# Half of an input product as seven block products per chunk in place of eight, with the rounding of the weight blocks shared by two engines

## The chip, the cores and the metric

One core of a Trainium2 chip runs the whole program. The metric is the device time in microseconds, a median over runs. Engines: TensorE (PE) multiplies, VectorE (DVE), ScalarE (ACT) and GpSimd (POOL) work on elements, SyncE (SP) issues the transfers.

## The reference

Two residual blocks on x of shape (1, 1024, 1024), all in float32. The first is the one touched:

```python
u = rms_norm(h, norm_in_g[l])
proj = jnp.einsum('bsd,de->bse', u, w_in[l])
pool_x, pool_z, m_x, m_z = jnp.split(proj, [D_POOL, 2 * D_POOL, 2 * D_POOL + D_MLSTM], axis=-1)
y_pool = pool_mixer(pool_x, pool_w[l], pool_scale[l]) * jax.nn.silu(pool_z)
y_m = mlstm_branch(m_x, ...) * jax.nn.silu(m_z)
y = jnp.concatenate([y_pool.astype(h.dtype), y_m.astype(h.dtype)], axis=-1)
h = h + jnp.einsum('bse,ed->bsd', y, w_out[l])
```

`pool_mixer` takes four groups of 256 features; in each it forms a centred window mean (over 2, 4, 8 or 16 positions) minus the value itself, and multiplies by a 256x256 matrix. The second block (gating, a 31-tap convolution, windowed attention) is not touched.

## The kernel before

Every large product is made in three passes. A float32 factor is split into a high part, rounded to the format that TensorE takes (`fp32r`), and a low part, the rest. `three` issues low x high, high x low and high x high into one PSUM bank, each a matmul of 128x512 columns.

Weights come in chunks of 256 output features, 1 MB each, into the one buffer `wraw` (`wt`, SP). GpSimd rounds a chunk into `whi` (L687) and subtracts it into `wlo` (L689), function `split`; both have two buffers. The pool half of `w_in` is eight chunks, two per group g: chunk 2g gives `pool_x` and chunk 2g+1 gives `pool_z`. For each, `group` makes four tiles (two of 128 features, two halves of 512 positions), each a sum over eight blocks k of 128 inputs: 4 x 8 x 3 = 96 matmuls.

The order around it is written out by hand in each engine's program, with semaphores between them:

- TensorE: chunk 0 in a special order (`lagging`, while x is still being transposed), then per g the chunks 2g and 2g+1 and the mixing, 4 x 2 x 3 = 24 matmuls, then the output product over y (chunks 8 to 11, 96 matmuls each), then chunk 12 (`W_MX`) and the rest.
- ScalarE: copies the tiles of chunk 2g out of PSUM to `px`, applies silu to those of chunk 2g+1 (`sz`), and rounds the pooled values and y.
- VectorE: at the start it scales x (L1511) and makes the low parts of u (L1520). Per g it forms the windows (L1555 to L1561, on `px`, in `pta` and `ptb`), the low parts of the mixing's factors (L1565, L1569), scales the mixing's result (L1578) and makes the low part of y (L1586).
- y lies as `yp_hi` and `yp_lo` in SBUF from the mixing to the output product, in the place where x was and, for the low part, beside it.

## Time and profile before

| | before |
|---|---|
| median of 3 runs | 1170.21 us (1169.76 to 1170.4) |
| span of the profiled execution | 1168.5 us |
| TensorE busy | 1158.7 us, 99% |
| TensorE weight loads | 946.1 us, 81%, beside the matmuls |
| VectorE busy | 678.5 us, 58% |
| GpSimd busy | 455.9 us, 39% |
| ScalarE busy | 359.2 us, 31% |
| DMA | 93.56 MB, 80 GB/s in the mean |

The span runs from the first to the last instruction; the profiled execution has no time of its own beside it, and the median of the runs lies 1.7 us above the span. A matmul's record ends later than the next one starts, so the pace of TensorE is read from the starts. The granted clock of TensorE is at its full level (2.4 GHz) in all 40 slices of the page.

### The profile page before, as it was taken

Reading aid. Unit: us, or ns where it says so; the run is one execution under the profiler, and the core shown is the slowest. Engines: PE = TensorE matmul, PEld = TensorE weight load, DVE = VectorE, ACT = ScalarE, POOL = GpSimd, SP = SyncE. Lnnn points to the kernel's source line nnn. Section 1 sums busy time; section 2 is a strip of 40 time slices with the busy share of each in tenths; the row PEclk is TensorE's granted clock in tenths of the full one; section 3 lists DMA queues with packets and bytes.
Section 4 is the critical chain, followed back from the end, with each engine's and each line's share of the span. In section 5 each row is a group of like instructions: output and inputs, shape, how many; then the busy total and the mean of one; then the engine's idle time right before and its main releaser. Section 6 shows DMA issues by size and latency. Waiting matters only on the chain.

```text
span 1168.5 us, 17252 instructions
## 1 busy us (share of the span) xinstructions
PE 1158.7 (99%) x6599; PEld 946.1 (81%) x6599; DVE 678.5 (58%) x1249; ACT 359.2 (31%) x720; POOL 455.9 (39%) x437
## 2 busy tenths in 40 slices
PE   9999999999999999999999999999999999999997
PEld 6888888888888868888878888878988887777786
DVE  5645557334368502157777883894699434556668
ACT  6312121100012212445665631242111134553322
POOL 2424222223333223354657656304223323455534
PEclk9999999999999999999999999999999999999999
DMA  7321121343312112300113242123121130133113
GB/s 241 109 81 45 36 81 36 123 152 114 109 36 72 64 64 90 101 23 23 50 34 112 88 171 73 72 100 95 40 88 36 37 100 1 38 122 124 39 38 141
DMA packets 75075, 93.56 MB, mean 80 GB/s; under 512 B 13938, under 2 KB 54090, under 8 KB 74483
## 3 DMA queue, kind: packets, MB, share of 16 engines
q1 hardware_dynamic: 67270, 88.73, 22.7%
q10 hardware_dynamic: 7724, 3.74, 1.2%
q8 instruction: 53, 0.87, 0.3%
q14 instruction: 28, 0.22, 0.1%
HBM read 75.11 MB, written 18.92 MB: 80 GB/s over the span
## 4 chain that ended last, share of the span: by engine, by line
PE 93%; DVE 4%; DMA 1%; ACT 1%; issue 1%; POOL 0%; ACTq 0%; DVEq 0%; POOLq 0%
PE bank L918 22%; PE bank L920 22%; PE bank L919 22%; PE bank L1219 4%; PE bank L1194 4%; PE wide L1210 2%; PE wide L1412 2%; PE bank L1158 1%; PE bank L1147 1%; PE bank L1135 1%; PE wide L920 1%; PE wide L919 1%; PE wide L918 1%; PE bank L1387 1%; DVE h L1910 1%; PE wide L1387 1%
## 5 line engine op out<-in xcount | busy, mean ns | idle before, releaser
L687 POOL CAST whi<-wraw 128x2048 fp32r<-128x2048 f32 x31 | 58.8, 1898 | 454.1 <-PE bank L920 404.1
L918 PE MATMUL bank<-u_hi,wlo 128*128 128x512 f32 x488 | 190.4, 390 | 0.0
L920 PE MATMUL bank<-u_hi,whi 128*128 128x512 f32 x488 | 189.9, 389 | 0.0
L919 PE MATMUL bank<-u_lo,whi 128*128 128x512 f32 x488 | 189.9, 389 | 0.0
L689 POOL TENSOR_TENSOR wlo<-wraw,whi 128x2048 fp32r<-128x2048 f32 x32 | 153.1, 4784 | 3.0 <-ACT whi L2488 0.5
L918 PE MATMUL bank<-x_hi,wlo 128*128 128x512 f32 x312 | 123.5, 396 | 0.0
L920 PE MATMUL bank<-x_hi,whi 128*128 128x512 f32 x312 | 121.6, 390 | 0.0
L919 PE MATMUL bank<-x_lo,whi 128*128 128x512 f32 x312 | 121.5, 389 | 0.0
L918 PEld LDWEIGHTS bank<-u_hi,wlo 128*128 128x128 f32 x488 | 91.6, 188 | 19.9 <-POOL wlo L689 0.8
L920 PEld LDWEIGHTS bank<-u_hi,whi 128*128 128x128 f32 x488 | 91.6, 188 | 19.0
L919 PEld LDWEIGHTS bank<-u_lo,whi 128*128 128x128 f32 x488 | 91.6, 188 | 18.9
L918 PEld LDWEIGHTS bank<-x_hi,wlo 128*128 128x128 f32 x312 | 58.5, 188 | 16.1 <-issue 4.3
L1990 DVE SCALAR_TENSOR_TENSOR wide<-glu,VT,wide 128x1024 f32<-128x1024 f32 x58 | 69.3, 1281 | 0.0
L920 PEld LDWEIGHTS bank<-x_hi,whi 128*128 128x128 f32 x312 | 58.5, 188 | 12.4
L919 PEld LDWEIGHTS bank<-x_lo,whi 128*128 128x128 f32 x312 | 58.6, 188 | 11.7
L862 POOL TENSOR_SCALAR sp<-sp,rcx 128x384 f32<-128x384 f32 (+1 forms) x64 | 37.9, 606 | 76.4 <-DVE rcx L2077 76.4
L1219 PE MATMUL bank<-v,kwb 128*128 128x257 f32 x224 | 58.3, 383 | 0.5 <-DVE Cst L1773 0.3
L1650 DVE SCALAR_TENSOR_TENSOR cva<-um,VT,cva 128x1022 f32<-128x1022 f32 (+1 forms) x32 | 58.0, 1812 | 1.1
L1194 PE MATMUL bank<-Cst,qT 128*128 128x257 f32 x224 | 58.0, 381 | 0.1
L2296 ACT ACTIVATE um<-bank 128x512 f32<-128x512 f32 x16 | 9.6, 599 | 155.7 <-PE bank L920 155.7
L783 POOL TENSOR_TENSOR Pm<-ST,Wb 128x128 f32<-128x128 f32 x64 | 29.1, 455 | 66.0 <-ACT Wb L2368 61.2
L918 PE MATMUL bank<-whi,ym_lo 128*128 128x512 f32 x128 | 51.2, 400 | 0.0
(391 smaller groups left out, 2440.9 us busy)
## 6 DMA issues: line engine op xcount, KB each, us to landing
wraw<-in_w_in SPq DMA_DIRECT2D x26, 1024.0 KB, 5.5
wraw<-in_w_out SPq DMA_DIRECT2D x12, 1024.0 KB, 5.1
xr<-in_x SPq DMA_DIRECT2D x8, 512.0 KB, 7.3
hst<-in_x SPq DMA_DIRECT2D x4, 1024.0 KB, 5.0
hpool<-hst SPq DMA_DIRECT2D x4, 1024.0 KB, 4.1
smz<-mzs SPq DMA_DIRECT2D x16, 256.0 KB, 2.0
h<-hpool SPq DMA_DIRECT2D x4, 1024.0 KB, 7.5
resid<-h SPq DMA_DIRECT2D x8, 512.0 KB, 2.6
```

The lines of the kernel that those rows point to most:

```text
L687: g_.tensor_copy(whi[w % 2][:, :, :], wraw[:, :, :]).then_inc(s["w_hi"], 1)
L689: g_.tensor_tensor(wlo[w % 2][:, :, :], wraw[:, :, :], whi[w % 2][:, :, :].bitcast(F32), ALU.subtract).then_inc(s["w_lo"], 1)
L783: g_.tensor_tensor(Pm[:, n % 2, :], STs[h % 2][:, ck, :], Wb[:, n % 2, :], ALU.mult).then_inc(s["g_P"], 1)
L862: g_.tensor_scalar(row, row, rcx[:, x % 2, i:i + 1], 0.5 if g else 1.0, ALU.mult, ALU.mult).then_inc(s["g_nm"], 1)
L918: pe.matmul(ps, al, bh, start=(k == 0), stop=False)
L919: pe.matmul(ps, ah, bl, start=False, stop=False)
L920: return pe.matmul(ps, ah, bh, start=False, stop=(k == nk - 1))
L1194: mm = pe.matmul(ps[:, 0:AUG], q[:, k, ck * P:(ck + 1) * P], Cst[:, d, k, :], start=(k == 0), stop=(k == 1))
L1210: pe.matmul(ps[:, 0:AUG], Pm[:, n % 2, :], v[:, ck, :], start=True, stop=True).then_inc(s["t_intra"], 1)
L1219: mm = pe.matmul(ps[:, 0:AUG], kwb[:, m % 2, k * P:(k + 1) * P], v[:, ck, :], start=True, stop=True)
L1650: ins = ve.scalar_tensor_tensor(acc[:, a0:a1], um[:, j, a0 + sh:a1 + sh], tap(q), acc[:, a0:a1], ALU.mult, ALU.add)
L1990: ins = ve.scalar_tensor_tensor(dst, src, w, acc, ALU.mult, ALU.add)
```

## The change

For chunks 1 to 7 (`SEVEN`), a product of two by two blocks is made of seven block products. The blocks are those of the inputs (k 0 to 3 and 4 to 7, called 0 and 1), of the features (two of 128) and of the positions (two halves of 512). Each product has inner length 4 x 128 and makes 4 x 3 = 12 matmuls: 84 a chunk. Three of the seven use the halves of u as they are (0 and 1 in the first half, 1 in the second), four use sums and differences of them, `Tf`, made once. Of the seven weight blocks, three are blocks of the raw weights, which ScalarE rounds; four are sums and differences or one raw difference, which GpSimd forms and rounds itself; the low parts of all seven are GpSimd's. VectorE adds the seven results to four tiles (`add_up`, one operand in PSUM, `p1s` or `p5s` in SBUF). Slots for eight blocks lie in the old weight buffers.

To make room, y is stored to DRAM when it is made (`store_y`) and read back before the output product (`load_y`); four blocks of u's second half are parked in DRAM too (`late_d`). A chunk's weights come as two halves of 512 KB (`halves`), each when its place in `wraw` is free. The mixing of group g now comes after the second product of chunk 2g+2; that of group 3 after chunk 7.

```diff
+    for w, (_, _, layout) in enumerate(plan):
+        first.append(first[-1] + (0 if w in SEVEN else size[layout]))
...
+            def halves(c, f):
+
+                if c == 1:
+                    sp_.wait_ge(s["w_lo"], 1)
+                else:
+                    sp_.wait_ge(s["w_lo"] if f else s["g_m0"], c if f else c - 1)
...
+            for c in range(2, 8):
+                for f in range(2):
+                    halves(c, f)
+                if c % 2:
+                    g = (c - 3) // 2
+                    store_y(g)
+                    sp_.wait_ge(s["t_mix"], 4 * g + 4)
+                    mix_weights(g + 1)
+            wt(W_OP)
...
-            g_.wait_ge(s["v_xn"], NT)
-            for w in range(1, W_MX + 2):
+            g_.wait_ge(s["v_ulo"], 8)
+            for n in range(2):
+                ks = slice(4 * n, 4 * n + 4)
+                g_.tensor_tensor(Tf[:, 2 + n, :, :], u_hi[:, ks, 0:HALF].bitcast(F32), u_lo[:, ks, 0:HALF].bitcast(F32),
+                                 ALU.add).then_inc(s["g_T"], 1)
...
+            def seven(c):
+
+                b0 = 7 * (c - 1)
+
+                def low(i, src):
+                    return g_.tensor_tensor(slot(wlo, b0 + i), src, slot(whi, b0 + i).bitcast(F32), ALU.subtract)
...
+                for k in range(2):
+                    g_.wait_ge(s["a_wa"], 3 * c - 2 + k)
+                    low(k, raw(0, k)).then_inc(s["g_blk"], 1)
+                g_.wait_ge(s["l_wraw"], 16 * (c + 1))
+                x = xs[:, :, :]
+                step(g_.tensor_tensor(x, raw(1, 0), raw(1, 1), ALU.add))
+                step(g_.tensor_tensor(raw(1, 0), raw(0, 0), raw(1, 0), ALU.subtract))
+                part(2, x).then_inc(s["g_blk"], 1)
+                g_.wait_ge(s["g_blk"], 6 * (c - 1) + 3)
+                step(g_.tensor_tensor(x, x, raw(0, 0), ALU.subtract))
+                part(3, x).then_inc(s["g_blk"], 1)
+                g_.wait_ge(s["g_blk"], 6 * (c - 1) + 4)
+                g_.tensor_tensor(x, raw(0, 1), x, ALU.subtract).then_inc(s["g_m0"], 1)
+                g_.wait_ge(s["g_m0"], c)
+                part(4, x).then_inc(s["g_blk"], 1)
+                part(5, raw(1, 0)).then_inc(s["g_blk"], 1)
+                g_.wait_ge(s["a_wa"], 3 * c)
+                low(6, raw(1, 1)).then_inc(s["w_lo"], 1)
...
+            def seven(c):
+
+                b0, v0 = 7 * (c - 1), 7 * (c - 1)
+                features = lambda k, nh: [u[:, 4 * k:4 * k + 4, nh * HALF:(nh + 1) * HALF] for u in (u_hi, u_lo)]
+                combined = lambda i: [T[:, i, :, :] for T in (Thi, Tlo)]
+                factors = (features(0, 0), features(1, 0), combined(0), combined(1), features(1, 1), combined(2),
+                           combined(3))
...
+                    if i < 6:
+                        pe.wait_ge(s["g_blk"], 6 * (c - 1) + i + 1)
+                    else:
+                        pe.wait_ge(s["w_lo"], c + 1)
+                    if c == 1 and i in LATE_T:
+                        pe.wait_ge(s["v_Tlo"], LATE_T[i])
+                    wh, wl = slot(whi, b0 + i), slot(wlo, b0 + i)
+                    for k in range(4):
+                        mm = three(ps[:, :], ((wh[:, k, :], wl[:, k, :]), (moving[0][:, k, :], moving[1][:, k, :])),
+                                   k, 4)
+                    mm.then_inc(s["t_prod"], 1)
+                    if i == 1 and c % 2 == 0:
+                        mix(c // 2 - 1)
...
+            ve.wait_ge(s["v_ulo"], 16)
+            whole(0, 0)
+            ve.wait_ge(s["g_T"], 2)
+            combine(0, full(0), full(2), ALU.subtract)
+            whole(1, 1)
+            combine(1, full(1), full(0), ALU.subtract)
+            low_T(0)
+            combine(2, full(1), full(2), ALU.subtract)
+            combine(3, full(3), full(1), ALU.subtract)
+            low_T(1)
...
+            for c in SEVEN:
+                g = c // 2
+                if c < 7:
+                    high_block(c + 1, 0)
+                if c > 1:
+                    keep(c)
+                if c < 7:
+                    high_block(c + 1, 1)
```

GpSimd after its first subtractions, before the change: one cast and one subtraction of 2048 columns for each chunk (L708 and L702 belong to chunk 0).

```order
L702 TENSOR_TENSOR wlo<-wraw,whi 128x2x128 x4
L687 CAST whi<-wraw 128x2048
L689 TENSOR_TENSOR wlo<-wraw,whi 128x2048
L687 CAST whi<-wraw 128x2048
L689 TENSOR_TENSOR wlo<-wraw,whi 128x2048
```

The same place after the change: first the two additions for `Tf` (L807), then the first eleven operations for chunk 1 (L822 low parts, L830 casts, L838 to L845 sums and differences of weight blocks in `xs`).

```order
L807 TENSOR_TENSOR Tf<-u_hi,u_lo 128x2048 x2
L822 TENSOR_TENSOR wlo<-wraw,whi 128x512 x2
L838 TENSOR_TENSOR xs<-wraw 128x512
L839 TENSOR_TENSOR wraw<-wraw 128x4x128
L830 CAST whi<-xs 128x512
L822 TENSOR_TENSOR wlo<-xs,whi 128x512
L842 TENSOR_TENSOR xs<-xs,wraw 128x512
L830 CAST whi<-xs 128x512
L822 TENSOR_TENSOR wlo<-xs,whi 128x512
L845 TENSOR_TENSOR xs<-wraw,xs 128x512
L830 CAST whi<-xs 128x512
L822 TENSOR_TENSOR wlo<-xs,whi 128x512
```

Two operations of 2048 columns per chunk became fifteen of 512, and two of 2048 stand ahead of them. VectorE at the end of u's low parts, before:

```order
L1511 TENSOR_SCALAR xr<-xr,rs 128x1024
L1520 SCALAR_TENSOR_TENSOR u_lo<-wide0,VT,u_hi 128x512 x2
L1520 SCALAR_TENSOR_TENSOR u_lo<-wide1,VT,u_hi 128x512 x2
L1520 SCALAR_TENSOR_TENSOR u_lo<-wide0,VT,u_hi 128x512 x2
L1520 SCALAR_TENSOR_TENSOR u_lo<-wide1,VT,u_hi 128x512 x2
L1539 COPY VT<-wide0 128x144
L1555 TENSOR_TENSOR pta<-px 128x1055
L1559 TENSOR_TENSOR pta<-pta,cst 128x8
L1560 TENSOR_TENSOR pta<-pta,cst 128x8
```

And after, up to the first window for group 0 (L1742 makes the four `Tf`, L1751 their low parts, L1735 is `add_up`):

```order
L1695 SCALAR_TENSOR_TENSOR u_lo<-wide1,VT,u_hi 128x512 x2
L1742 TENSOR_TENSOR Tf<-u_hi,u_lo 128x2048
L1742 TENSOR_TENSOR Tf<-Tf 128x2048
L1742 TENSOR_TENSOR Tf<-u_hi,u_lo 128x2048
L1742 TENSOR_TENSOR Tf<-Tf 128x2048
L1751 TENSOR_TENSOR Tlo<-Tf,Thi 128x2048
L1742 TENSOR_TENSOR Tf<-Tf 128x2048 x2
L1751 TENSOR_TENSOR Tlo<-Tf,Thi 128x2048
L1766 COPY VT<-wide0 128x144
L1735 TENSOR_TENSOR sz<-wide1,p1s 128x512
L1751 TENSOR_TENSOR Tlo<-Tf,Thi 128x2048 x2
L1822 TENSOR_TENSOR pta<-px 128x1055
```

Ten operations of 2048 columns stand between the last low part of u and the first window. VectorE ahead of the mixing of group 3, before (L1555 to L1561 the windows of the second 128 features, then the low parts; L1578 follows the mixing):

```order
L1555 TENSOR_TENSOR pta<-px 128x1055
L1555 TENSOR_TENSOR ptb<-pta 128x1053
L1555 TENSOR_TENSOR pta<-ptb 128x1049
L1555 TENSOR_TENSOR ptb<-pta 128x1041
L1559 TENSOR_TENSOR ptb<-ptb,cst 128x8
L1560 TENSOR_TENSOR ptb<-ptb,cst 128x8
L1561 SCALAR_TENSOR_TENSOR px<-ptb,px 128x1024
L1565 TENSOR_TENSOR pwlo<-pw,pwhi 128x512
L1569 TENSOR_TENSOR yp_lo<-px,yp_hi 128x1024 x2
L1578 SCALAR_TENSOR_TENSOR yr<-wide,VT,sz 128x512 x2
```

The same place after the change, with `add_up` of chunk 7 (L1735) between the windows and the low parts:

```order
L1822 TENSOR_TENSOR pta<-px 128x1055
L1822 TENSOR_TENSOR ptb<-pta 128x1053
L1735 TENSOR_TENSOR sz<-wide,p1s 128x512
L1822 TENSOR_TENSOR pta<-ptb 128x1049
L1822 TENSOR_TENSOR ptb<-pta 128x1041
L1829 TENSOR_TENSOR ptb<-ptb,cst 128x8
L1830 TENSOR_TENSOR ptb<-ptb,cst 128x8
L1831 SCALAR_TENSOR_TENSOR px<-ptb,px 128x1024
L1837 TENSOR_TENSOR pwl<-pw,pwhi 128x512
L1841 TENSOR_TENSOR pxl<-px,u_hi 128x1024
L1735 TENSOR_TENSOR p5s<-wide,p1s 128x512
L1735 TENSOR_TENSOR p1s<-wide,p5s 128x512
```

The windows are the same. What moved: the mixing's low parts (now `pwl` and `pxl`) stand among the additions of chunk 7's products, one of which (L1735) is already inside the windows, and the mixing waits for the second `pxl`.

## Rows read from the trace of the kernel before

**Rows 1.** The page: span and busy time of each engine

```profile
span 1168.5 us, 17252 instructions
...
PE 1158.7 (99%) x6599; PEld 946.1 (81%) x6599; DVE 678.5 (58%) x1249; ACT 359.2 (31%) x720; POOL 455.9 (39%) x437
```

**Rows 2.** TensorE's waits, longest first: who for, us, times, longest

```profile
PE bank L960 <- POOL eps L694: 1.0, 1, 1.0
```

**Rows 3.** TensorE's timeline: start us, us, engine, line, what

```profile
41.09 0.47 PE L918 MATMUL bank<-u_hi,wlo 128*128 128x512 f32 x1
...
209.85 0.39 PE L918 MATMUL wide<-yp_hi,pwlo 128*128 128x512 f32 x1
...
214.61 0.39 PE L918 MATMUL wide<-yp_hi,pwlo 128*128 128x512 f32 x1
```

**Rows 4.** GpSimd's timeline, in three stretches

```profile
43.26 5.50 POOL L689 TENSOR_TENSOR wlo<-wraw,whi 128x2048 fp32r<-128x2048 f32 x1
63.27 1.89 POOL L687 CAST whi<-wraw 128x2048 fp32r<-128x2048 f32 x1 [14.51 <-PE bank L920]
65.24 4.61 POOL L689 TENSOR_TENSOR wlo<-wraw,whi 128x2048 fp32r<-128x2048 f32 x1
...
835.83 4.61 POOL L689 TENSOR_TENSOR wlo<-wraw,whi 128x2048 fp32r<-128x2048 f32 x1
...
1015.43 0.61 POOL L843 CAST whi<-wraw 128x512 fp32r<-128x512 f32 x1
1016.13 1.27 POOL L846 TENSOR_TENSOR wlo<-wraw,whi 128x512 fp32r<-128x512 f32 x1
```

**Rows 5.** VectorE's timeline, in two stretches

```profile
41.92 2.37 DVE L1555 TENSOR_TENSOR pta<-px 128x1055 f32<-128x1055 f32 x1 [0.29 <-ACT px L2241]
44.33 4.46 DVE L1559 TENSOR_TENSOR pta<-pta,cst 128x8 f32<-128x8 f32 x1
48.82 0.17 DVE L1560 TENSOR_TENSOR pta<-pta,cst 128x8 f32<-128x8 f32 x1
...
65.89 0.75 DVE L1578 SCALAR_TENSOR_TENSOR yr<-wide,VT,sz 128x512 f32<-128x512 f32 x1 [0.53 <-PE wide L920]
66.56 3.85 DVE L1586 TENSOR_TENSOR yp_lo<-yr,yp_hi 128x512 fp32r<-128x512 f32 x1
...
71.11 0.68 DVE L1586 TENSOR_TENSOR yp_lo<-yr,yp_hi 128x512 fp32r<-128x512 f32 x1
...
837.60 2.87 DVE L1997 TENSOR_SCALAR v_<-mv 128x8 f32<-128x8 f32 x1
```

**Rows 6.** The timeline of all engines at the start

```profile
19.93 0.74 POOL L702 TENSOR_TENSOR wlo<-wraw,whi 128x256 fp32r<-128x256 f32 x1
...
20.44 0.78 DVE L1511 TENSOR_SCALAR xr<-xr,rs 128x1024 f32<-128x1024 f32 x1
...
21.81 0.76 DVE L1511 TENSOR_SCALAR xr<-xr,rs 128x1024 f32<-128x1024 f32 x1
...
23.59 0.48 PEld L1026 LDWEIGHTS wide<-cst,xr 128*128 128x128 f32 x3
...
25.31 0.49 PEld L1026 LDWEIGHTS wide<-cst,xr 128*128 128x128 f32 x3
...
34.02 1.08 ACT L2241 ACTIVATE px<-bank 128x512 f32<-128x512 f32 x2
```

**Rows 7.** VectorE's groups by shape, 0 to 330 us: count | busy, mean ns

```profile
L1569 DVE TENSOR_TENSOR yp_lo<-px,yp_hi 128x1024 fp32r<-128x1024 f32 x8 | 9.5, 1219 | 0.2 <-ACT yp_hi L2279 0.2
...
L1555 DVE TENSOR_TENSOR ptb<-pta 128x1041 f32<-128x1041 f32 x2 | 2.5, 1247 | 0.1
```

**Rows 8.** The page's DMA issues: KB each, us to landing

```profile
wraw<-in_w_in SPq DMA_DIRECT2D x26, 1024.0 KB, 5.5
...
smz<-mzs SPq DMA_DIRECT2D x16, 256.0 KB, 2.0
```

**Rows 9.** DMA issues from 0 to 330 us

```profile
wraw<-in_w_in SPq DMA_DIRECT2D x2, 512.0 KB, 10.2
```

More of the change, by code:

```diff
@@ L104, in chunk_plan @@
     return plan
+SEVEN = range(1, 8)
 def build(nc, I, out):
@@ L110, in build @@
     first = [0]
-    for _, _, layout in plan:
-        first.append(first[-1] + size[layout])
+    for w, (_, _, layout) in enumerate(plan):
+        first.append(first[-1] + (0 if w in SEVEN else size[layout]))
     NCH = len(plan)
@@ L235, in build @@
         (_k, vrow, vrow2, junk, relst, hot,
-         px, pta, ptb, sz, yr, pw, pwhi, pwlo,
+         px, pta, ptb, sz, yr, pw, pwhi, xs,
+         pxl, _z, yl, pwl,
          hst,
@@ L527, in _ @@
                 load_h(0, q)
+            wt(W_OP + 1)
+            store_y(3)
+            for i in range(2):
+                sp_.wait_ge(s[f"o_y{i}"], 256)
+            sp_.wait_ge(s["t_prod"], products + 7)
+            load_y(4, slice(0, S), "l_yc")
+            load_y(6, slice(0, S), "l_yc")
+            sp_.wait_ge(s["v_sum"], 7 * len(SEVEN))
+            for part, (u, sl) in enumerate(((u_hi, slice(0, 4)), (u_lo, slice(0, 4)))):
+                sp_.dma_start(u[:, sl, HALF:S].bitcast(F32), late_d[:, part, :, :]).then_inc(s["l_late"], 16)
             wt(W_OP + 2)
@@ L833, in _ @@
                 split(w)
-            parts = [7]
             def split_part(w, part):
@@ L1556, in _ @@
                         src = dst
+                        if g and step == 1:
+                            for i in (0,) if m else (4, 5, 6):
+                                add_up(2 * g + m, i)
                     tot = src[:, PAD - left:PAD - left + S]
@@ L1596, in fold_gates @@
                         ve.wait_ge(s["l_wg"], 16 * 12)
+                        ve.wait_ge(s["w_lo"], W_OP)
+                        for i in range(2):
+                            ve.wait_ge(s[f"o_y{i}"], 256)
                     w = wn[:, :, :, :].rearrange("p n j o -> p (n j o)").unsqueeze(2).to_broadcast([P, 96, 8])
@@ new lines, in _ @@
+            for k in range(2):
+                high_block(1, k)
+            for i in range(3):
+                pooled(0, i)
+            high_T(0)
+            high_T(1)
+            pooled(0, 3)
+            ac.wait_ge(s["o_late"], 32)
+            high_T(2)
+            high_last(1)
+            high_T(3)
+            keep(1)
+            for c in SEVEN:
+                g = c // 2
+                if c < 7:
+                    high_block(c + 1, 0)
+                if c > 1:
+                    keep(c)
+                if c < 7:
+                    high_block(c + 1, 1)
+                if c % 2 == 0:
+                    for n in range(4):
+                        high_y(4 * (g - 1) + n)
+                    high_last(c + 1)
+                    continue
+                ac.wait_ge(s["l_pw"], 16 * (g + 1))
@@ L2288, in conv_silu @@
+                if c < 7:
+                    high_last(c + 1)
+            for n in range(12, 16):
+                high_y(n)
             def conv_silu(j):
```

354 lines of the change are left out of this document (251 added, 103 removed).

## The prediction

> **What bounds the kernel now.** Read the page first: TensorE is busy for 1158.7 of 1168.5 us [rows 1]. The list of waits is next: TensorE's longest wait anywhere is 1.0 us, at the very start [rows 2]. Then its timeline: from 209.85 to 214.61 us there are 21 steps between starts, 0.2267 us for each 128x512 matmul [rows 3] (the 389 ns of a record is the modelled, overlapping length, so only starts count). So TensorE's instruction count sets the end, at 0.2267 us a piece, as long as nobody makes it wait. The question is what the change takes off that count, and whether the other engines still deliver in time.
>
> **What is removed.** Seven chunks go from 4 groups x 8 x 3 = 96 matmuls to 7 products x 4 x 3 = 84. That is 84 fewer, 84 x 0.2267 = **19.0 us**. The mixing products (24 a pair of chunks) stay. A chunk now takes 19.0 us, a product 2.72, a mixing 5.4; a pair of chunks with its mixing 43.5.
>
> **What is added, and the resource that it needs.** GpSimd did one cast (63.27: 1.89 us) and one subtraction (65.24: 4.61 us) per chunk [rows 4]. Now it does 11 two-input operations and 4 casts of 128x512 each. Rows of that size, late in the program, have 0.61 and 1.27, and I take 1.28 with the step between two [rows 4]: 11 x 1.28 + 4 x 0.61 = 16.5 us a chunk, 33.0 a pair. That alone is under TensorE's 43.5. What matters is with whom it is shared. At 44.33 VectorE starts an addition of 8 columns, whose twin at 48.82 takes 0.17 us; it takes 4.46 us and ends at 48.79, just when GpSimd's subtraction ends (43.26 + 5.50 = 48.76) [rows 4, 5]. At 66.56 a subtraction that takes 0.68 us when free (71.11) takes 3.85 and ends 0.56 us after GpSimd's (65.24 + 4.61 = 69.85). It goes the other way too: GpSimd's 4.61 is 5.50 where VectorE was in an operation until 44.29 (41.92 + 2.37). But the operation at 65.89, which reads PSUM, keeps its 0.75 us inside the same GpSimd subtraction. So operations of VectorE whose operands all lie in SBUF and GpSimd's operations exclude one another, for their whole length; one that waited is shortened by about 0.13 us (0.56 for 0.69; 48.76 - 44.29 = 4.47 for 4.61).
>
> The Trainium skill states this in "SBUF — State Buffer", section "SBUF: two separate sides": a port pair that the two engines share is an exclusive lock, and whichever starts first has it for the whole instruction. By that rule without the 0.13 us, the waits below would sum to about 15 us more, and the time would be some 1218 us. The trace agrees with the rule but for those 0.13 us, and the sum goes by the trace.
>
> I therefore wrote down the five engines' instructions of the stage in the new order, each with its duration from these rows and started when its semaphores allow, and gave the port to whoever asked first. Each place where TensorE waits is a term.
>
> *a. Start.* GpSimd's two 2048-column additions follow its first subtractions, at 20.67 (19.93 + 0.74) [rows 6]. VectorE is scaling x just then: its 0.78 us operation at 20.44 holds the port until 21.2, the addition runs to 25.7, and the scaling that was issued at 21.81 ends at 26.3. TensorE wants that tile at 23.59: **2.7 us**. The second addition runs to 30.8, the next scaling to 31.4; TensorE, 2.7 us late, is there at 28.0: **3.3 us**. The last tile comes in time. Whether a scaling, one input in SBUF, is held too, no row in this stretch shows; the bound below is 0. I take the full price, since a one-input operation of 8 columns, started at 837.60, lasts 2.87 us, to the end of GpSimd's subtraction of 835.83 [rows 4, 5].
>
> *b. Chunk 1.* It started at 41.1 [rows 3], now at 47.1; its fifth product would start at 47.1 + 4 x 2.72 = 58.0. That product needs GpSimd's twelfth operation. GpSimd starts when ScalarE is through (34.02 [rows 6] + 6.0 + 0.6 = 40.6), and from there it alternates with VectorE's ten 2048-column operations (two of 1.22 [rows 7], less one overhead, give 2.25 each) and one window. So 9 x 1.28 + 3 x 0.61 + 10 x 2.25 + 1.25 = 37.1, less 22 handovers x 0.13 = 34.2: ready at 74.8. **16.8 us** of waits, spread over products 3 to 5. Bounds: 1.8 us if the port were free, some 20 without the 0.13.
>
> *c. Chunks 2 to 7.* In a pair VectorE needs, all from SBUF: two windows of g+1 additions (1.25 each), small edges (0.17), one scaling of 1024 (1.23), pwl (0.69), two pxl (1.22) and four yl (0.69) [rows 5, 7], 14.0, 16.5 and 19.0 us for g = 1, 2, 3. With GpSimd's 33.0 that is 47.0, 49.5 and 52.0, less 34 to 42 handovers x 0.13 = 42.6, 44.6, 46.5, against TensorE's 43.5. The 14 additions of products read PSUM, so they don't ask for the port (0.69 each, the length of the twin from SBUF), but they queue behind operations that do. There is no slack left, so each late result shows: chunk 2 waits 1.9 and 5.4 us for its first product to be copied and added up, since ScalarE is held by a weight half still in flight and VectorE by what it left from chunk 1; chunks 4 and 6 wait 0.4 + 1.4 and 3.6 for the mixing's operands. **12.7 us**. I took 4.0 us for the landing of a 512 KB half, between 2.0 (256 KB) and 5.5 (1 MB) [rows 8]; at 3.0 the total is 3.6 us less, at 5.5 it is 5 us more.
>
> *d. The last mixing.* Chunk 7 ends, and the windows for g = 3 have only begun with that chunk: 13.1 us of port time for windows, 3.1 for the low parts, 9 of additions, and GpSimd's last blocks and the first 4.6 us subtraction for the output product between them. **11.5 us**. Before, the same windows lay beside a whole chunk, with GpSimd's 6.5 us.
>
> *e. y by way of memory.* y is now stored and read back. The first half is read during chunk 7. Of the second, four reads of 1 MB follow the last stores; at about 2.9 us each in a queue (the 5.5 us of one alone, less the part that overlaps, an estimate) they land some 4.6 us after TensorE has spent its 21.8 us on the first output chunk. **4.6 us**, bounds 0 and 10. ScalarE's three casts per chunk (0.6 us each, as its two copies in 1.08 us at 34.02 [rows 6]) don't use the port and lie beside TensorE's 19 us: nothing; put on GpSimd they would add 1.8 us of port a chunk.
>
> *Sum:* 6.0 + 16.8 + 12.7 + 11.5 + 4.6 = 51.6 us of waits, less 19.0: +32.6. The span would be 1168.5 + 32.6 = 1201.1; the median of the runs, 1170.21, lies 1.7 above the span, and I keep that: **1203 us**.
>
> **The rivals.** *R1, only the start and the end show* (0.15): in the steady stretch whoever asks does not lose as much as I think, and c and d fall away to about 0 and 4. Then 6.0 + 16.8 + 4 + 4.6 - 19.0 = +12, or with the start's 6.0 absent too, +6: 1176 to 1183. For it: port time and TensorE time are nearly equal in c (42.6 to 46.5 against 43.5). Against it: d's windows come last whatever the pairs do. *R2, faster* (0.13): the two engines seldom meet, because their requests interleave in the gaps that each has at semaphores. The same order without any exclusion leaves waits of 1.8 us in chunk 1 and 4.6 for y, 6.4 - 19.0 = -12.6: 1157.6 us. It decides the sign once all waits together stay under 19.0 us, that is, if less than four tenths of mine come true. Against it: the ten 2048-column operations and GpSimd's twelve stand in one stretch with nothing else to do, b alone is 16.8. *R3, transfers* (0.07): 512 KB halves in 512-byte pieces land as late as the two at the start, whose median is 10.2 us [rows 9], and GpSimd stands idle for each: 12 halves, of whose extra 6 us about a third is hidden, over +20 on top: 1222 and above. *R4, no change* (0.02): waits happen to be 19.
>
> **How the numbers follow.** My own case has 0.63, with 1184 to 1222 as its range: the waits at the low side (handover 0.2 us, halves in 3 us, nothing for y) sum to 33, at the high side (no handover gain, halves in 5.5) to 71. Adding R1 brings the range to 1174 to 1222, which holds 0.78. A measurement of this kernel can tell 0.2% (2.3 us) from no change. Faster than that: R2, 0.13. Within: 0.02. Slower: 0.63 + 0.15 + 0.07 = 0.85.
>
> **What would show it.** In the profile of the changed kernel: TensorE's waits should sum to about 50 us, with 2 to 4 us each on the scaled x at 24 to 31 us (a), on GpSimd's blocks in chunk 1 (b), and a single wait over 8 us on pxl before the last mixing (d). VectorE's 2048-column operations should last about 3.3 us from issue, not 2.25, and GpSimd's 512-column ones in 41 to 75 us over 3 us. The matmuls should be 84 fewer at the same 0.2267 us. I am wrong if VectorE's operations from SBUF run at their own length beside GpSimd's (then R2), if chunk 1 ends before about 70 us, or if the longest waits are on transfers (R3).

## The result and the profile after

| | before | after |
|---|---|---|
| median | 1170.31 us (1169.76 to 1170.95, 4 runs) | 1215.25 us (1213.83 to 1217.47, 4 runs) |
| profiled execution | span 1168.5 us | 1216.29 us, span 1214.5 us |
| mean granted clock of TensorE | 0.999 | 0.976 |

The ratio is 1.0389, 95% interval 1.0374 to 1.0404: 44.9 us slower where 33 were forecast. First the page of the changed kernel, to be read beside [rows 1]: the span, the busy times, TensorE's 40 slices and those of its granted clock.

```profile
span 1214.5 us, 17418 instructions
...
PE 1160.2 (96%) x6515; PEld 942.2 (78%) x6515; DVE 762.9 (63%) x1308; ACT 373.1 (31%) x732; POOL 577.4 (48%) x530
...
PE   8878999687999999999999999999999999999997
...
PEclk9878999898999999999999999999999999999999
```

The 84 matmuls are gone (6599 to 6515), and still TensorE is busy as long as before. TensorE's two dips (slices 2 to 4 and 8 to 10) lie in the first ten slices, and its granted clock falls in five of these six. Next TensorE's list of waits, which had a longest entry of 1.0 us before [rows 2]: who waits for whom, us in total, times, longest. `PE bank L1057 <- DVE pxl` is a matmul that writes `bank` and waited for VectorE's `pxl`.

```profile
PE bank L1057 <- DVE pxl L1841: 11.2, 2, 10.2
PE bank L1057 <- DMA yp_lo<-ylow: 8.9, 1, 8.9
PE bank L1057 <- POOL wlo L822: 7.3, 2, 3.7
PE wide L1057 <- POOL wlo L822: 5.1, 1, 5.1
PE wide L1165 <- DVE xr L1686: 4.9, 2, 2.6
PE wide L1057 <- DVE px L1735: 4.8, 1, 4.8
PE wide L1057 <- issue: 3.4, 1, 3.4
```

These ten waits sum to 45.6 us. But a wait is not all that is lost at its place, because matmuls behind it run slower. What is lost is read from starts. This is TensorE's timeline at the ends of the prediction's five terms: chunk 1 begins, its product 5 (the last late one) begins, the third mixing, the last mixing, the second output chunk, and the first matmul of `W_MX`.

```profile
48.06 0.47 PE L1057 MATMUL wide<-u_hi,wlo 128*128 128x512 f32 x1
...
76.23 0.77 PE L1057 MATMUL bank<-u_hi,wlo 128*128 128x512 f32 x1 [3.60 <-POOL wlo L822]
...
188.41 0.50 PE L1057 MATMUL bank<-u_hi,pwl 128*128 128x512 f32 x1 [0.98 <-DVE pxl L1841]
...
237.11 0.80 PE L1057 MATMUL bank<-u_hi,pwl 128*128 128x512 f32 x1 [10.23 <-DVE pxl L1841]
...
281.21 0.79 PE L1057 MATMUL bank<-whi,yp_lo 128*128 128x512 f32 x1 [8.92 <-DMA yp_lo<-ylow]
...
349.22 0.39 PE L1057 MATMUL bank<-u_hi,wlo 128*128 128x512 f32 x1
```

Between two of them, the elapsed time less 0.2267 us for each matmul is the loss. Chunk 1 began at 41.09 before [rows 3]; `W_MX` began at 302.33, by TensorE's timeline in the kernel before:

```profile
302.33 0.39 PE L918 MATMUL bank<-u_hi,wlo 128*128 128x512 f32 x1
```

| term | stretch | matmuls | lost | forecast |
|---|---|---|---|---|
| a start | to 48.06 | as before | 7.0 | 6.0 |
| b chunk 1 | to 76.23 | 48 | 17.3 | 16.8 |
| c chunks 2 to 7 | to 188.41 | 444 | 11.5 | 12.7 |
| d last mixing | to 237.11 | 168 | 10.6 | 11.5 |
| e y by way of memory | to 349.22 | 408 | 19.6 | 4.6 |

The sum is 66.0, less 19.0 for the 84 matmuls: +47.0, and `W_MX` began 46.9 us later. The third mixing stands inside chunk 6, so what chunks 6 and 7 lose behind it is booked under d. Four terms came within 1.2 us of their forecast; e is 15 us too small. The mechanism that carries a to d can be seen directly, at the start and in chunk 1. VectorE's timeline (answering to [rows 5, 6]):

```profile
20.23 0.75 DVE L1686 TENSOR_SCALAR xr<-xr,rs 128x1024 f32<-128x1024 f32 x1
...
21.60 4.36 DVE L1686 TENSOR_SCALAR xr<-xr,rs 128x1024 f32<-128x1024 f32 x1
...
26.07 4.84 DVE L1686 TENSOR_SCALAR xr<-xr,rs 128x1024 f32<-128x1024 f32 x1
...
48.47 3.28 DVE L1742 TENSOR_TENSOR Tf<-u_hi,u_lo 128x2048 f32<-128x2048 f32 x1
51.78 3.26 DVE L1742 TENSOR_TENSOR Tf<-Tf 128x2048 f32<-128x2048 f32 x1
55.07 2.58 DVE L1751 TENSOR_TENSOR Tlo<-Tf,Thi 128x2048 fp32r<-128x2048 f32 x1
...
67.08 0.69 DVE L1735 TENSOR_TENSOR sz<-wide,p1s 128x512 f32<-128x512 f32 x1
```

And GpSimd's in the same stretch, against [rows 4], where such operations take 0.61 and 1.27:

```profile
41.70 4.58 POOL L822 TENSOR_TENSOR wlo<-wraw,whi 128x512 fp32r<-128x512 f32 x2 [11.34 <-ACT whi L2527]
46.25 3.34 POOL L838 TENSOR_TENSOR xs<-wraw 128x512 f32<-128x512 f32 x1
49.67 3.22 POOL L839 TENSOR_TENSOR wraw<-wraw 128x512 f32<-128x512 f32 x1
52.95 2.55 POOL L830 CAST whi<-xs 128x512 fp32r<-128x512 f32 x1
...
62.13 2.55 POOL L830 CAST whi<-xs 128x512 fp32r<-128x512 f32 x1
64.76 3.19 POOL L822 TENSOR_TENSOR wlo<-xs,whi 128x512 fp32r<-128x512 f32 x1
```

The two engines take turns: each operation lasts as long as its own work and that of the other engine which ran first. One pair takes 3.30 us (48.47 to 51.78 to 55.07). The addition `sz<-wide,p1s`, one operand in PSUM, keeps its 0.69 us inside GpSimd's operation of 64.76.

### The profile page after: what moved, and what is told of

Its sections match the earlier page's. It is cut to its first block, busy times and chain, and to the rows that moved or that the text cites. A ratio compares the mean times of both kernels' runs of the same rounds, so it can differ in the third digit from the quotient of the medians.

```text
span 1214.5 us, 17418 instructions
## 1 busy us (share of the span) xinstructions
PE 1160.2 (96%) x6515; PEld 942.2 (78%) x6515; DVE 762.9 (63%) x1308; ACT 373.1 (31%) x732; POOL 577.4 (48%) x530
## 4 chain that ended last, share of the span: by engine, by line
PE 78%; DVE 10%; POOL 5%; DMA 3%; issue 2%; ACT 1%; SPq 1%; DVEq 0%; ACTq 0%; POOLq 0%
PE bank L1057 19%; PE bank L1059 18%; PE bank L1058 18%; PE bank L1369 3%; PE bank L1394 3%; DMA ylow<-yl 2%; PE wide L1385 2%; PE wide L1587 2%; DVE pta L1822 1%; POOL wlo L822 1%; DVE px L1831 1%; DVE ptb L1822 1%; DVE yl L1788 1%; PE bank L1333 1%; PE bank L1322 1%
## 5 line engine op out<-in xcount | busy, mean ns | idle before, releaser
L779 POOL CAST whi<-wraw 128x2048 fp32r<-128x2048 f32 x24 | 45.5, 1894 | 353.8 <-PE bank L1059 284.2
L1057 PE MATMUL bank<-x_hi,wlo 128*128 128x512 f32 x312 | 123.5, 396 | 0.0
L1057 PE MATMUL bank<-u_hi,wlo 128*128 128x512 f32 x300 | 118.3, 394 | 3.6 <-POOL wlo L822 3.6
L781 POOL TENSOR_TENSOR wlo<-wraw,whi 128x2048 fp32r<-128x2048 f32 x25 | 117.2, 4688 | 2.4 <-ACT whi L2804 0.5
L1059 PE MATMUL bank<-u_hi,whi 128*128 128x512 f32 x300 | 117.7, 392 | 0.0
L1058 PE MATMUL bank<-u_lo,whi 128*128 128x512 f32 x300 | 117.7, 392 | 0.0
L1057 PEld LDWEIGHTS bank<-x_hi,wlo 128*128 128x128 f32 x312 | 58.6, 188 | 16.1 <-issue 4.3
L1057 PEld LDWEIGHTS bank<-u_hi,wlo 128*128 128x128 f32 x300 | 56.8, 189 | 16.6 <-issue 4.0
L1059 PEld LDWEIGHTS bank<-u_hi,whi 128*128 128x128 f32 x300 | 56.9, 190 | 12.0
L1058 PEld LDWEIGHTS bank<-u_lo,whi 128*128 128x128 f32 x300 | 56.9, 190 | 11.7
L924 POOL TENSOR_TENSOR Pm<-ST,Wb 128x128 f32<-128x128 f32 x64 | 30.0, 469 | 66.0 <-ACT Wb L2684 61.2
L1057 PE MATMUL bank<-whi,yp_lo 128*128 128x512 f32 x112 | 44.8, 400 | 8.9 <-DMA yp_lo<-ylow 8.9
```

The source lines that it names most:

```text
L779: g_.tensor_copy(whi[w % 2][:, :, :], wraw[:, :, :]).then_inc(s["w_hi"], 1)
L781: g_.tensor_tensor(wlo[w % 2][:, :, :], wraw[:, :, :], whi[w % 2][:, :, :].bitcast(F32), ALU.subtract).then_inc(s["w_lo"], 1)
L924: g_.tensor_tensor(Pm[:, n % 2, :], STs[h % 2][:, ck, :], Wb[:, n % 2, :], ALU.mult).then_inc(s["g_P"], 1)
L1057: pe.matmul(ps, al, bh, start=(k == 0), stop=False)
L1058: pe.matmul(ps, ah, bl, start=False, stop=False)
L1059: return pe.matmul(ps, ah, bh, start=False, stop=(k == nk - 1))
```

## The experiments

All differences are between medians, against the 1215.25 us of the changed kernel. The kernel before, run again beside each, had medians of 1169.8 to 1170.2, so a median moves by about 0.4 us from one set of runs to the next; the single runs of one kernel spread by 1 to 6 us, and what this leaves of a difference is said where it matters.

### GpSimd's first additions later

```diff
             g_.wait_ge(s["v_ulo"], 8)
+            g_.wait_ge(s["v_xn"], NT)
             for n in range(2):
```

> GpSimd's two additions of 2048 columns at the start (the first combined factors) wait until VectorE has scaled all of x; nothing else changes. If GpSimd's additions hold back VectorE's scaling through the port that the two share: TensorE's two waits at the start (2.4 and 3.0 us in the profile after) fall under 0.5 us each, the scaling steps keep their 0.5 us distance, and the time falls by 5 to 8 us (the waits, and the low clock at 30 to 35 us), less what the later additions delay of chunk 1. If the engines do not hold each other back: the two waits stay and the time is that of the changed kernel within 1 us, or 1 to 2 us more.

1208.65 us, ratio to the kernel before 1.0333 (1.0318 to 1.0348): **6.6 us less**. VectorE's timeline in this run:

```profile
21.61 0.76 DVE L1687 TENSOR_SCALAR xr<-xr,rs 128x1024 f32<-128x1024 f32 x1
...
22.98 0.76 DVE L1687 TENSOR_SCALAR xr<-xr,rs 128x1024 f32<-128x1024 f32 x1
...
24.35 0.76 DVE L1687 TENSOR_SCALAR xr<-xr,rs 128x1024 f32<-128x1024 f32 x1
```

The scaling is back at 0.76 us and both waits at the start are gone. Nothing of VectorE's was touched: the port theory holds here, for an operation with one tensor input too. The Trainium skill, "SBUF — State Buffer", section "SBUF: two separate sides", lists VectorE's operations with two SBUF inputs and those in a two-port mode among those that take the lock. The trace agrees for the first kind; of the scaling, with one, it shows that it was held, and no row here names its mode.

### VectorE's four low parts of the factors away

ScalarE writes plain copies in their place, so the values of the four low parts are not those of the reference.

```diff
-            low_T(0)
...
-            low_T(1)
...
-            low_T(2)
-            low_T(3)
...
+                ac.activation(Tlo[:, i, :, :], Tf[:, i, :, :], ACT.Copy).then_inc(s["v_Tlo"], 1)
```

> The low parts of the four combined factors are not computed: ScalarE writes a plain bf16 copy of the combined factor in their place, so VectorE's four subtractions of 2048 columns are gone from chunk 1 (this part of the computation is changed, the values of the low parts are not those of the reference). If chunk 1's waits come from VectorE and GpSimd taking turns at one port: TensorE's three waits of chunk 1 (5.25, 4.1 and 3.8 us), which the trace puts down to GpSimd's blocks, shrink although GpSimd's own instructions are unchanged; the sum of the three falls by 6 to 9 us and the time by 7 to 12 with the clock. If each engine is bound by its own work: GpSimd's blocks come when they came, and the time stays within 2 us.

1207.98 us, ratio 1.0326 (1.0310 to 1.0343): **7.3 us less**. GpSimd's timeline in this run, whose program is the same:

```profile
62.05 0.61 POOL L830 CAST whi<-xs 128x512 fp32r<-128x512 f32 x1
62.74 1.28 POOL L822 TENSOR_TENSOR wlo<-xs,whi 128x512 fp32r<-128x512 f32 x1
```

Up to 62 us it goes step for step as in the changed kernel. Then VectorE has nothing to do (no operation of its own from 61.2 to 69.7), and the cast takes 0.61 for 2.55, the subtraction 1.28 for 3.19. Of TensorE's three waits in chunk 1 the first keeps its 5.1 us, the second is 0.9 for 3.7, and the third is gone; a new one of 4.5 us stands before the first mixing. What the list of waits calls GpSimd's block is as much VectorE's work.

### Who rounds the three raw blocks

All casts on GpSimd (`e3_casts_gpsimd`), the second half of the change undone; in `e12_first_casts` only those of chunk 1:

```diff
                 for k in range(2):
+                    if c == 1:
+                        g_.wait_ge(s["l_w0"], 32)
+                        g_.tensor_copy(slot(whi, k), raw(0, k)).then_inc(s["a_wa"], 1)
                     g_.wait_ge(s["a_wa"], 3 * c - 2 + k)
...
+                if c == 1:
+                    g_.wait_ge(s["t_gemm"], 4)
+                    g_.tensor_copy(slot(whi, 6), raw(1, 1)).then_inc(s["a_wa"], 1)
...
-            for k in range(2):
-                high_block(1, k)
...
-            high_last(1)
```

> Undoes the second half of the change: the high parts of blocks 0, 1 and 6 of each chunk are rounded on GpSimd again, ahead of their subtractions; ScalarE rounds none. My prediction priced these casts at 1.8 us of shared port a chunk. If chunk 1 is bound by the port throughout, GpSimd's work grows by three casts there and the time by 2 to 10 us (1217 to 1225); if the waits of chunk 1 are set by VectorE's sums, or if ScalarE is itself late with block 6, the casts fit in GpSimd's idle time and the time is the same within 1.5 us.

1217.24 us, ratio 1.0408 (1.0393 to 1.0424): 2.0 us more, at the low edge of the 2 to 10 expected, and hardly clear of the spread of the runs (1216.96 to 1218.75 against 1213.83 to 1217.47). But the time had moved: product 5 of chunk 1 began at 69.86, 6.4 us earlier than in the changed kernel (71.24 and 5.0, which stand in the next expectation, were read six matmuls too late in the product), and a wait of 5.8 us came up before the first mixing. Two effects of opposite sign, so the two were parted:

> The changed kernel, with the high parts of chunk 1's three blocks rounded on GpSimd and those of chunks 2 to 7 on ScalarE. In the profile after, GpSimd stands idle for 11.3 us until 41.70, because ScalarE rounds the first two blocks only behind its casts of u; with all casts on GpSimd (the run e3_casts_gpsimd) it went on at once, product 5 of chunk 1 began 5.0 us earlier (71.24 for 76.23), and the time was still 2.0 us more. If ScalarE's lateness costs these 5 us and the port price of the later casts gave them back: this hybrid keeps product 5 near 71, loses nothing later, and takes 1208 to 1212. If what chunk 1 gains is always given back by VectorE's later work (the wait before the first mixing, 6.0 us in that run, where the profile after has none): 1213 to 1217.

1207.89 us, ratio 1.0318 (1.0302 to 1.0334): **7.4 us less** than the changed kernel. GpSimd's timeline of this run:

```profile
30.33 1.07 POOL L836 CAST whi<-wraw 128x512 fp32r<-128x512 f32 x1
31.48 1.60 POOL L822 TENSOR_TENSOR wlo<-wraw,whi 128x512 fp32r<-128x512 f32 x1
33.02 0.61 POOL L836 CAST whi<-wraw 128x512 fp32r<-128x512 f32 x1
```

It starts on chunk 1 at 30.33, not at 41.70, while VectorE is on operands in PSUM. Product 5 begins at 70.70, and 4.4 us of wait before the first mixing remain. So moving the casts of chunks 2 to 7 to ScalarE is worth 1217.24 - 1207.89 = 9.4 us, 1.6 us a chunk in the mean, and moving those of chunk 1 costs 7.4 us, since ScalarE comes late there. The 9.4 us are not spread evenly. The four mixings began at 89.43, 134.64, 185.63 and 237.76 with all casts on GpSimd, and at 88.90, 134.77, 179.78 and 228.28 here: chunks 2 and 3 gained nothing, and the gain lies behind the second mixing, where with all casts on GpSimd TensorE waited 3.2 us in chunk 4 and 2.4 us in chunk 6.

### The output weight's split behind the last windows

```diff
                 if w != W_2:
+                    if w == W_OP:
+                        g_.wait_ge(s["v_px"], 20)
```

> GpSimd's splitting of the first output weight block (a cast of 1.90 and a subtraction of 4.51 us, at 224.30 in the profile after) waits until VectorE's windows of the last group are done; nothing else changes. There the profile after shows an addition of 8 columns of 1.90 us and a scaling of 1024 columns of 5.42 us, whose twins take 0.17 and 1.23: 5.9 us. If this is the port, both go back to their own length, the 10.4 us wait before the last mixing falls to 4 to 6 us, and the time by 4 to 6 us, less up to 1.5 us of a new wait for the weight block. If the wait has another origin: the time stays within 1 us.

1207.42 us, ratio 1.0323 (1.0308 to 1.0339): **7.8 us less**, more than the 4 to 6 expected. VectorE in the changed kernel, while GpSimd splits (224.30 to 230.8):

```profile
224.32 1.90 DVE L1829 TENSOR_TENSOR ptb<-ptb,cst 128x8 f32<-128x8 f32 x1
...
226.46 5.42 DVE L1831 SCALAR_TENSOR_TENSOR px<-ptb,px 128x1024 f32<-128x1024 f32 x1
```

and in this run:

```profile
225.51 0.17 DVE L1831 TENSOR_TENSOR ptb<-ptb,cst 128x8 f32<-128x8 f32 x1
...
225.92 1.23 DVE L1833 SCALAR_TENSOR_TENSOR px<-ptb,px 128x1024 f32<-128x1024 f32 x1
```

The wait before the last mixing fell from 10.2 to 2.8 us. From the third mixing to the last TensorE took 42.8 us (189.57 to 232.39) for 48.7: 5.9 us of the gain lie in this stretch, the rest behind it.

### The stores of y ahead of the loads, and y read back in two parts

```diff
+            store_y(3, range(2))
             sp_.wait_ge(s["t_mix"], 16)
...
             wt(W_OP + 1)
-            store_y(3)
+            store_y(3, range(2, 4))
```

> The two stores of y of tile 12 and 13 (four transfers) are issued ahead of the 3 MB that SyncE now puts before them (two loads of x, 1 MB each, and a weight block); same transfers, same data. In the profile after, VectorE waits 12.7 us for these stores (until 257.49) before it may write y of the next two tiles, TensorE waits 3.4 us at 259.60 for the PSUM bank of one of them, and 8.9 us at 281.21 for y. If the order in the queue is the cause of both: VectorE goes on at about 248 to 250, the 3.4 us wait is gone, that of 8.9 falls under 4, and the time falls by 7 to 11 us. If the transfers of y are bound by their volume instead: the wait moves to the loads of x or the weight block, and the time falls by 0 to 3 us.

1206.37 us, ratio 1.0310 (1.0293 to 1.0327): **8.9 us less**. SyncE's issues in the changed kernel show the order: two loads of x and a weight block, 3 MB, stand just ahead of the first stores.

```profile
245.38 0.93 SPq L600 DMA_DIRECT2D hst<-in_x  x2
246.35 0.51 SPq L497 DMA_DIRECT2D wraw<-in_w_out  x1
246.91 0.80 SPq L566 DMA_DIRECT2D yhigh<-u_lo  x1
247.74 0.47 SPq L567 DMA_DIRECT2D ylow<-yl  x1
```

VectorE's next step in the changed kernel:

```profile
257.49 0.75 DVE L1782 SCALAR_TENSOR_TENSOR yr<-wide,VT,sz 128x512 f32<-128x512 f32 x1 [12.73 <-DMA ylow<-yl]
```

and with the stores first:

```profile
246.67 0.75 DVE L1783 SCALAR_TENSOR_TENSOR yr<-wide,VT,sz 128x512 f32<-128x512 f32 x1 [2.03 <-DMA ylow<-yl]
```

The stores are issued only 3.0 us earlier (243.87 for 246.91), but the first two have landed 10.8 us earlier (VectorE goes on at 246.67 for 257.49). TensorE's 3.4 us wait at 259.60 is gone. The list gave no releaser for it (`issue`); that it was for the PSUM bank which this step reads follows from this run, and from the run with idle products below, where those at this place wait 3.5 us for VectorE's `yr`. The wait for y is 5.0, not 8.9, somewhat more than the "under 4" expected. The other half of the same path:

```diff
+            for i in range(2):
+                sp_.wait_ge(s[f"o_y{i}"], 192)
+            sp_.wait_ge(s["t_prod"], products + 6)
+            load_y(4, slice(0, S), "l_yc")
...
-            load_y(4, slice(0, S), "l_yc")
```

> The pooled y of group 2 is read back as soon as chunk 7 lets its place go; only that of group 3 is read after its own stores, so 2 MB instead of 4 stand behind the last store. In the profile after, the reads begin at 268.86 and TensorE goes on at 281.21, after a wait of 8.9 us. If the wait is the length of these reads: it falls to 3 to 5 us, and the time by 4 to 6 us. If it is set by when the last stores are issued (263.25 to 265.03), the first reads bring no more than 2 us, and the reads of 2 MB may put the loads behind them later.

1209.75 us, ratio 1.0340 (1.0325 to 1.0356): **5.5 us less**, as expected; the wait for y is 2.5 us.

### TensorE kept at work through its waits

```diff
+                if g == 3:
+                    free = turn[0] % 8
+                    pe.wait_ge(s[last[free][0]], last[free][1])
+                    fill(bank[free], 11)
                 pe.wait_ge(s["v_px"], 5 * g + 5)
```

and the like at eight other places (the expectation speaks of ten waits and lists nine).

> TensorE gets idle products (a 128x128 tile of ones, fp32, 512 columns, about 0.85 us each, into a bank that is free anyway) ahead of ten of its waits: 3 and 5 at the start, 5, 4 and 4 in chunk 1, 5 in chunk 2, 11 before the last mixing, 3 and 9 before the products that read y. They take the place of waiting and change no operand. Theory A (about 18 us of the 44.9 us are TensorE at the low level of the granted clock in the stretches around its waits, and the waits themselves are 47 us): the slices at .5 to .8 around those places go to full, the waits stay, and the span falls by 8 to 18 us, to about 1197 to 1207. Rival B (the low clock lies where TensorE waits for blocks anyway, and costs nothing on the path): the slices go to full and the time stays within 3 us of 1215. Rival C (the fillers are late and are waited for): slower than 1215.

1212.58 us, ratio 1.0363 (1.0337 to 1.0389): 2.7 us less, which the spread of the runs (1208.97 to 1215.15 against 1213.83 to 1217.47) does not set clear of nothing; the span of the profiled execution is 3.9 less. Two windows of the changed kernel: length, then each engine's busy time, the granted clock, the DMA share and GB/s.

```profile
60.00:80.00 20.00, 12.69 (x32) 9.17 (x31) 19.76 (x13) 7.55 (x8) 19.55 (x9) 0.67 0.09 27
280.00:300.00 20.00, 18.79 (x71) 15.35 (x72) 3.46 (x5) 0.00 (x0) 6.50 (x2) 0.83 0.87 260
```

and the same of this run:

```profile
60.00:80.00 20.00, 17.11 (x53) 10.39 (x52) 19.76 (x13) 7.46 (x8) 19.55 (x9) 0.91 0.09 27
280.00:300.00 20.00, 20.00 (x90) 16.53 (x89) 4.84 (x7) 0.00 (x0) 6.51 (x2) 1.00 0.75 206
```

The clock rose to 0.994 in the mean, and most of the 18 us that I had put down to it did not come back. The result is that of rival B, within 3 us of 1215, and not the 8 to 18 us of theory A. In chunk 1 VectorE and GpSimd have the same 19.76 and 19.55 us in the window, and TensorE, faster, waits longer for the same blocks. Chunk 1 began at 46.94, product 5 at 75.03, the third mixing at 187.23 and the last at 235.73. Up to the last mixing TensorE still waited 0.2 to 2.7 us behind each group of idle products, so they held nothing up there, and only 1.4 us had been gained (235.73 for 237.11).

For the last place that does not hold. TensorE's timeline in this run:

```profile
272.21 7.89 PE L1105 MATMUL bank<-ones 128*128 128x512 f32 x18
279.54 0.79 PE L1057 MATMUL bank<-whi,yp_lo 128*128 128x512 f32 x1
```

The last read of y was issued at 265.05 and landed 10.9 us later, at 276.0; the nine idle products ran until 279.54. They ran 3.5 us too long, which is rival C at this one place. (The three ahead of the wait for the PSUM bank, at 255.96, began only when the bank was free and ran past it too; the wait for y behind them hides that.) The second output chunk began 1.7 us earlier than in the changed kernel (279.54 for 281.21), and `W_MX` 4.0 (345.26 for 349.22); without the overlong filling it could have been some 7 us (an estimate, 4.0 + 3.5). So the low clock costs 1.4 us on the path up to the last mixing, and up to some 6 us behind it, where fewer waits take the gain back.

### Four edits together

The additions later, the split later, the stores first, y in two parts.

> Four edits together: GpSimd's first additions after the scaling of x, the split of the output weight after the last windows, y of group 2 read early, the stores of y ahead of the loads. If each takes away a wait of its own place, the gains add up: the 6.6 us measured for the first, 4 to 6, 7 to 11 and 1 to 3 for what is left of the reads, together 18 to 25 us, so 1190 to 1197. If the waits only move from one place to the next: the gain is no more than that of the largest, about 1205.

1186.96 us, ratio 1.0148 (1.0133 to 1.0164): 28.3 us less, more than the 18 to 25 expected. The four alone gave 6.6 + 7.8 + 8.9 + 5.5 = 28.8, so they add up, the two on the path of y too, although these share one stretch; as a pair alone they were not run. What is left in TensorE's list of waits is 18.2 us in chunks 1 and 2, and 5.4 us for `pxl`, 4.4 of them before the last mixing.

### Chunk 1 multiplied as before

`SEVEN = range(2, 8)`, on top of the four edits; 72 matmuls are saved, 16.3 us.

> The four edits of the run before, and chunk 1 multiplied as in the kernel before (four groups of 24 matmuls, 96), so that only chunks 2 to 7 take seven products: 72 fewer matmuls than before instead of 84, 16.3 us. The combined factors are then made beside chunk 1 (21.8 us that TensorE spends on it), not ahead of their first use. If the 13.8 us of waits in chunk 1 and the 5.2 in chunk 2 come from this preparation alone: they go, 2.7 us of matmuls come back, and the time is 1187 - 19.0 + 2.7, and 0 to 3 less by the clock: 1168 to 1171, level with the kernel before or 2 us ahead of it. If VectorE and GpSimd, who then share the port with chunk 1's split as well, are still behind in chunk 2: waits of 3 to 8 us there, 1172 to 1179.

1178.60 us, ratio 1.0082 (1.0067 to 1.0097): the second case by the time, but not by the waits, of which 3 to 8 us had been expected. One wait of 15.4 us at 83.45, for `pxl` before the first mixing, which stood last in VectorE's list. So the list was put in the order of use, and on SyncE's list the weights of chunk 2 were put ahead of the 2 MB that are saved of u (both in one run, so what each of them gave is not parted):

```diff
-            combine(2, full(1), full(2), ALU.subtract)
-            ve.wait_ge(s["g_T"], 2)
-            combine(3, full(3), full(1), ALU.subtract)
-            low_T(1)
...
+                if g == 0:
+                    ve.wait_ge(s["g_T"], 2)
+                    combine(3, full(3), full(1), ALU.subtract)
+                    low_T(1)
+                    low_T(2)
```

> As the run before, with VectorE's and SyncE's order changed for chunk 2: the windows of group 0 and the low parts of the mixing's operands come ahead of the third and fourth combined factor and of the low parts of the second to fourth (in the run before, TensorE waited 15.4 us at 83.45 for the low part of px, which stood behind all of them); and the weights of chunk 2 are loaded ahead of the 2 MB that are saved of u (they landed at 50.0 there, 13.9 us after their issue). The same work on each engine. If the wait was only the order of VectorE's list: the operands are ready at 68 to 71, where TensorE arrives at 67.9, the later factors are each ready within 1 or 2 us of their use, and the time is 1178.6 less 11 to 15: 1163 to 1168, faster than the kernel before. If VectorE's and GpSimd's port work in the stretch is more than it holds in any order, the wait moves to the combined factors of products 3 to 7 of chunk 2, and the time is 1170 to 1176.

1176.07 us, ratio 1.0053 (1.0039 to 1.0067): 2.5 us less, where 11 to 15 were hoped for: the second case, that the stretch is too full in any order. And once more, two steps moved:

```diff
+                if g == 0:
+                    add_up(c, 0)
                 mixed(n)
                 mixed(n + 1)
```

> As the run before, with two steps of VectorE moved: the first sum of chunk 2 is made ahead of the mixing's results (TensorE waited 5.7 us at 93.88 for the PSUM bank that it sets free, and it stood behind two results that waited for stores), and the third combined factor behind the low parts of px (TensorE waited 4.0 us at 72.62 for these). If both waits were order: they shrink to 1 to 3 us together, the stretch at half clock behind them goes too, and the time falls by 7 to 10 us, to 1166 to 1169, level with the kernel before or just faster. If VectorE is simply full from 35 to 100 us: the wait moves to the last combined factors (products 6 and 7 of chunk 2) and the gain is 2 to 4 us, 1172 to 1174.

1175.65 us, ratio 1.0060 (1.0046 to 1.0073), no difference from the run before that can be told, and less than the 2 to 4 us of the second case. The window of this run points to a reason, and the list of waits where the 15.4 us have gone:

```profile
36.00:95.00 59.00, 57.53 (x254) 46.90 (x253) 56.46 (x31) 20.28 (x24) 52.62 (x26) 1.00 0.37 125
```

```profile
PE bank L1067 <- DVE pxl L1850: 6.8, 3, 2.8
PE bank L1067 <- DVE px L1748: 4.7, 1, 4.7
PE bank L1067 <- DMA yp_lo<-ylow: 1.8, 1, 1.8
PE wide L1067 <- DVE pxl L1850: 1.4, 1, 1.4
```

VectorE is in an operation for 56.46 of 59 us, GpSimd for 52.62, each partly blocked by the other. My reading is that any order only chooses which product waits; that no third order would do better is not shown. `W_MX` begins at 308.31, 6.0 us later than before, with 16.3 us of matmuls fewer. No version here beats the kernel before.

## Why the prediction was right, and where it was off

**Direction, bound and mechanism**: right. TensorE lost more around its waits than the 84 matmuls gave (19.0 us), and four of five terms came within 1.2 us. The exclusion of VectorE's SBUF operations and GpSimd's was the disputed step, and rival R2 (none of it, 1157.6 us) fell with the runs on the additions, the low parts and the split: each time the untouched engine went back to its own durations. The 0.13 us of a handover holds too: VectorE's 2.29 us (alone, in the run with chunk 1 as before) and GpSimd's 1.28 make 3.57, a pair takes 3.30, two handovers 0.27. By the rule of the Trainium skill ("SBUF — State Buffer") without that gain I had worked out 1218, nearer to the result; but what was missing lies in term e, and b, which has most of the handovers, came out at 17.3 for 16.8.

**How much of the agreement is luck**: the forecast's 47.0 us for a to d are waits at the full clock. The list has 33.3 us of waits there, and 13.1 us are slow matmuls, of which the prediction knew nothing. But the run with idle products, which held the clock up, lost 5.9, 17.2, 11.5 and 10.4 us in the same four stretches (45.0 for 46.4): with a faster TensorE the waits grow, so VectorE and GpSimd set these ends, as the terms say. What was luck is named under c.

**a, b**: 7.0 and 17.3 for 6.0 and 16.8. The full price for a one-input operation was right. The bound without a port for b, 1.8 us, is excluded. (Ahead of product 5 stand twelve operations of GpSimd, as b counts them; the list ahead of the prediction shows these twelve and calls them eleven.)

**c**: 11.5 for 12.7, in other places. Chunk 2 with what is left of chunk 1 lost 10.3 (7.3 forecast): one wait for a sum, 4.8 us, 2.4 of slow matmuls behind it, and 3.1 mostly behind the last wait of chunk 1; chunk 4 lost nothing, chunk 6 1.0 (5.4 forecast for the two). That the total fits is luck. R1 (c and d fall away, 1176 to 1183) is out: d was 10.6. Halves landed in 4.1 us (page, 16 of 512 KB), 4.0 taken, so R3 is out as well, for the weights.

**d**: 10.6 for 11.5. The run with the split later took 5.9 us off this stretch, so more than half of it is GpSimd's 6.5 us standing among the windows, as the term said. The 11.5 came out of the walk through the five engines' lists; the shares that the term names do not add up to it.

**e, the failed step**: "they land some 4.6 us after TensorE has spent its 21.8 us", with bounds 0 and 10. Measured: 19.6 us, outside both. From the start of the last mixing TensorE needs 5.4 + 21.8 = 27.2 us for it and the first output chunk, and the reads let it go on 16.9 us after that, not 4.6. The reads themselves took what I had counted: 12.3 us from 268.86 to 281.2, for 4 x 2.9 = 11.6. The step that failed is when they start: I took for given that the stores go out as y is made. They queue behind 3 MB on SyncE's list, VectorE waits 12.7 us for them since tiles 14 and 15 take the place of 12 and 13, one PSUM bank stays taken (3.4 us), and the reads start at 268.86. The 19.6 us are 12.3 us of waits, 4.6 us of slow matmuls up to 281.21 (2.6 of them in the last mixing, behind the wait of term d), and 2.7 behind. The two edits to this path gave back 8.9 and 5.5 us, and with both the list has 0.7 us of waits for y. The term is 15.0 us too small, where the whole sum lacked 14.3 at `W_MX` (46.9 for 32.6); the errors of the others nearly cancel.

**The casts on ScalarE "nothing"**: right for chunks 2 to 7, where they are a gain (1.6 us a chunk in the mean, for the 1.8 us of port taken, but all of it behind the second mixing), wrong for chunk 1. My own walk had GpSimd start "when ScalarE is through", and I booked this under the port; the run with the casts of chunk 1 on GpSimd took 7.4 us less.

**The granted clock** was no term of mine. Of the 66.0 us lost, 45.6 are waits; the other 20 are matmuls at the lower clock around them. With the clock held up, the path gave back 1.4 us up to the last mixing and 4.0 at `W_MX`, and some 7 by the estimate above. That keeps the terms a to d right although they were worked out at full speed; in e the clock has a share of its own.

**Open**: whether leaving chunks 2 and 3 as before too would tip the sum; the place of the mixing's factors lies in the second half of u, which those chunks would need, and it was not tried. What exactly makes the clock fall was not measured, nor the time with idle products that end before the data land.

## What to carry to other kernels

Saving matmuls on an engine that is 99% busy pays only as far as the other engines have room, and VectorE and GpSimd share theirs: add up their SBUF operations as one resource, stretch by stretch, before offloading work from TensorE. Where a result takes a way through memory, follow every transfer issued ahead of its store on the same queue, and who waits for the place that the store sets free. When a stall has been taken away by reordering and another of the same size comes up, look at the busy share of the engine in the whole stretch before trying a third order. An idle product that fills a wait must end before the wait would: compare its end with the landing of the data.
